# Up products with 512 columns of tokens, their halves added afterwards, and an earlier copy of the compressed keys

## The reference, cut to what matters

```python
def swiglu(h, w13, w2):
    a, b = jnp.split(h @ w13, 2, axis=-1)
    return (jax.nn.silu(a) * b) @ w2
```

## Time and profile before

| what | value |
|---|---|
| median of three runs | 1698.47 us |
| profiled execution | 1698.32 us, of which the span from the first to the last instruction is 1696.5 us |
| TensorE busy with matmuls | 1579.6 us, 93% |
| VectorE busy | 1104.0 us, 65% |
| ScalarE busy | 758.1 us, 45% |
| DMA | 327.31 MB, 193 GB/s in the mean |
| mean granted clock of TensorE | 0.966 of full |

### The profile page before, as it was taken

How to read it: one execution, slowest core, us unless ns; L and a number is a source line. 1 busy time by engine, 2 the same in 40 slices (tenths; PEclk the granted TensorE clock), 3 DMA queues, 4 the chain that set the end, 5 groups by cost and what they waited for, 6 DMA issues and landing times. The chain is left out here.

```text
span 1696.5 us, 24909 instructions
## 1 busy us (share of the span) xinstructions
PE 1579.6 (93%) x10338; PEld 1418.8 (84%) x10338; DVE 1104.0 (65%) x1571; ACT 758.1 (45%) x1144; POOL 22.9 (1%) x30
## 2 busy tenths in 40 slices
PE   5896879999999999999898999999999998989998
PEld 4684678999998999877777999889987777789986
DVE  3577655777776686568656677566776676567543
ACT  4634544343435444355535444354433655254442
POOL 0001000000000000000000000000000000000000
PEclk9998978999999999999889999999999998899999
DMA  7322324777674677544503677646775444156550
GB/s 257 112 76 111 127 100 171 283 275 292 255 285 155 234 281 273 215 166 170 184 28 122 242 267 269 255 177 244 263 283 191 160 176 149 32 187 242 173 201 35
DMA packets 56879, 327.31 MB, mean 193 GB/s; under 512 B 6448, under 2 KB 6832, under 8 KB 27312
## 3 DMA queue, kind: packets, MB, share of 16 engines
q1 hardware_dynamic: 55440, 322.76, 51.8%
q10 hardware_dynamic: 1328, 2.97, 0.5%
HBM read 324.65 MB, written 1.05 MB: 192 GB/s over the span
## 5 line engine op out<-in xcount | busy, mean ns | idle before, releaser
L286 DVE TENSOR_TENSOR wlo<-raw,whi 128x2048 fp32r<-128x2048 f32 (+2 forms) x236 | 533.8, 2265 | 281.8 <-ACT whi L281 281.6
L281 ACT ACTIVATE whi<-raw 128x2048 fp32r<-128x2048 f32 (+2 forms) x236 | 444.6, 1891 | 277.8 <-PE ps L1241 151.0
L1237 PE MATMUL ps<-hreg_r,whi 128*128 128x256 f32 x1760 | 501.0, 285 | 4.3 <-ACT mix L1286 4.3
L1241 PE MATMUL ps<-hreg_r,wlo 128*128 128x256 f32 x1760 | 500.0, 284 | 0.0
L1238 PE MATMUL ps<-hreg_r,whi 128*128 128x256 f32 x1760 | 500.0, 284 | 0.0
L1237 PEld LDWEIGHTS ps<-hreg_r,whi 128*128 128x128 f32 x1760 | 339.9, 193 | 5.7 <-ACT mix L1286 4.9
L1238 PEld LDWEIGHTS ps<-hreg_r,whi 128*128 128x128 f32 x1760 | 339.8, 193 | 0.5
L1241 PEld LDWEIGHTS ps<-hreg_r,wlo 128*128 128x128 f32 x1760 | 339.8, 193 | 0.0
L1386 PE MATMUL ps<-whi,ireg_r 128*128 128x512 f32 x480 | 187.4, 390 | 0.5 <-ACT ireg_r L1352 0.5
L1387 PE MATMUL ps<-whi,ireg_r 128*128 128x512 f32 x480 | 187.0, 390 | 0.0
L1390 PE MATMUL ps<-wlo,ireg_r 128*128 128x512 f32 x480 | 186.8, 389 | 0.0
(11 more groups left out here) (349 smaller groups left out, 1854.0 us busy)
## 6 DMA issues: line engine op xcount, KB each, us to landing
raw<-in_wu SPq DMA_DIRECT2D x230, 1024.0 KB, 5.6
adaw<-in_wada SPq DMA_DIRECT2D x144, 512.0 KB, 3.9
raw<-in_wu SPq DMA_DIRECT2D x4, 568.0 KB, 4.5
raw<-in_wu SPq DMA_DIRECT2D x2, 544.0 KB, 5.0
x<-in_x SPq DMA_DIRECT2D x2, 512.0 KB, 4.6
out<-hreg SPq DMA_DIRECT2D x2, 512.0 KB, 2.6
crow<-in_c ACTq DMA_DIRECT2D x1, 512.0 KB, 4.0
greg<-in_cst ACTq DMA_DIRECT2D x1, 512.0 KB, 8.3
```

Of the source, the lines that this page charges most:

```text
L281: act.activation(self.whi[:, m, 0:width], self.raw[:, n % NRAW, 0:width], ACT.Copy).then_inc(*self.A.done("hi", n))
L286: dve.tensor_tensor(self.wlo[:, m, 0:width], self.raw[:, n % NRAW, 0:width], self.whi[:, m, 0:width].bitcast(F32), ALU.subtract).then_inc( ...
L1237: pe.matmul(o, wh, self.hhi[:, kt, :], start=kt == 0, stop=False)
L1241: mm = pe.matmul(o, wl, self.hhi[:, kt, :], start=False, stop=kt == 7)
```

## The change

1. The upper and lower activations lie side by side, block by block: `hboth` is 8 x 512, and `hhi` and `hlo` are its halves.
2. In `up_tile` the two matmuls with `whi` become one with 512 columns. Its result has upper x upper in columns 0 to 255 of the bank and upper x lower in 256 to 511. The third matmul adds to the first half as before. Both tiles of a unit are made before the signal that it is done.
3. The two halves of the bank have to be added: ScalarE copies the second halves of both banks (`copy_act`, 128 x 512) into `sil` or `prd`, and VectorE adds the first halves to that (`sum_dve`, 128 x 512). Silu, gate, product, upper and lower part now run once for both tiles, with 512 elements, from and to SBUF. TensorE waits for the sum of the step before (`V("sum", ...)`) where it waited for silu or product.
4. The order on ScalarE and VectorE: `up_act` and `up_dve` replace the loops; the upper and lower part of a hidden product are made one step later, behind the next unit's split, and the `mod` operation is put before the split that it followed (`ada_first`).
5. `ada_table`: 1.00 per unit for the experts, 0.82 in the up units and 1.30 in the down units of a feed-forward stage; 0.60 in mixers as before. As a result the one that was due at VectorE's `ahead_dve(n0 + 14)` in either mixer is due at `ahead_dve(n0 + 15)`.
6. In `mixer_dve` the copies of the compressed keys and values stand before `ahead_dve(n0 + 14)`.

```diff
-            due += 60 if stage[n][0] == "m" else 96
+            due += 60 if stage[n][0] == "m" else 100 if stage[n][0] == "moe" else 130 if ORDER[n][0][0] == "w2" else 82
...
-        self.hhi = hr[:, 0:2048].rearrange("p (a b) -> p a b", b=256)
-        self.hlo = hr[:, 2048:4096].rearrange("p (a b) -> p a b", b=256)
+        self.hboth = hr[:, 0:4096].rearrange("p (a b) -> p a b", b=512)
+        self.hhi, self.hlo = self.hboth[:, :, 0:256], self.hboth[:, :, 256:512]
...
-            pe.matmul(o, wh, self.hhi[:, kt, :], start=kt == 0, stop=False)
-            pe.matmul(o, wh, self.hlo[:, kt, :], start=False, stop=False)
+            pe.matmul(self.ps[:, b, :], wh, self.hboth[:, kt], start=kt == 0, stop=False)
             if f == 0 and kt == 0:
                 pe.wait_ge(*V("lo", n))
-            mm = pe.matmul(o, wl, self.hhi[:, kt, :], start=False, stop=kt == 7)
+            mm = pe.matmul(self.ps[:, b, 0:256], wl, self.hhi[:, kt, :], start=False, stop=kt == 7)
...
-        for f in range(2):
-            pe.wait_ge(*A("sil", st, nth - 1, f))
-            mm = self.up_tile(pe, n, f, 4 + f)
-            mm.then_inc(*(P.done("up", st, nth, "a", 0) if f == 0 else P.done("unit", n)))
+        pe.wait_ge(*(A("sil", st, 0) if nth == 1 else V("sum", st, nth - 1, "a")))
+        self.up_tile(pe, n, 0, 4)
+        self.up_tile(pe, n, 1, 5).then_inc(*P.done("unit", n))
...
+    def up_act(self, act, name, j, st, nth, hi_before, free=None):
+        self.ahead_act(act, UNIT[name, "a", j])
+        if nth > 1:
+            self.hidden_act(act, st, nth - 1, hi_before, free)
+        self.copy_act(act, st, nth, "a", UNIT[name, "a", j], self.sil[:, nth % 2])
+        self.ahead_act(act, UNIT[name, "b", j])
+        self.silu_act(act, st, nth)
+        if nth > 2:
+            act.wait_ge(*self.V("hlo2", st, nth - 2))
+        self.copy_act(act, st, nth, "b", UNIT[name, "b", j], self.prd[:, nth % 2])
...
+    def copy_act(self, act, st, nth, part, n, to):
+        b = 4 if part == "a" else 6
+        act.wait_ge(*self.P("unit", n))
+        act.activation(to, self.ps[:, b:b + 2, 256:512], ACT.Copy).then_inc(*self.A.done("low", st, nth, part))
+
+    def sum_dve(self, dve, st, nth, part, to):
+        b = 4 if part == "a" else 6
+        dve.wait_ge(*self.A("low", st, nth, part))
+        dve.tensor_tensor(to, self.ps[:, b:b + 2, 0:256], to, ALU.add).then_inc(*self.V.done("sum", st, nth, part))
...
+    def up_dve(self, dve, name, j, st, nth, before, gate=None):
+        A, V = self.A, self.V
+        s, p = self.sil[:, nth % 2], self.prd[:, nth % 2]
+        self.ahead_dve(dve, UNIT[name, "a", j], True)
+        if nth > 1:
+            self.lower_dve(dve, st, nth - 1, *before)
+        self.sum_dve(dve, st, nth, "a", s)
+        self.ahead_dve(dve, UNIT[name, "b", j], True)
+        self.sum_dve(dve, st, nth, "b", p)
+        dve.wait_ge(*V("sum", st, nth, "b"))
         if gate is not None:
...
+            dve.tensor_tensor(p, p, gate.unsqueeze(1).to_broadcast([128, 2, 256]), ALU.mult).then_inc(*V.done("gated", st, nth))
+            dve.wait_ge(*V("gated", st, nth))
+        dve.wait_ge(*A("sil", st, nth))
+        dve.tensor_tensor(p, p, s, ALU.mult).then_inc(*V.done("prd", st, nth))
...
         maxima(7)
         probs(6)
-        self.ahead_dve(dve, n0 + 14)
         dve.wait_ge(*P("KC", st))
...
         dve.tensor_tensor(v["VC"], ps[:, 5, 64:128].unsqueeze(1).to_broadcast([128, 8, 64]),
                           self.bd.unsqueeze(2).to_broadcast([128, 8, 64]), ALU.mult).then_inc(*V.done("KC", st))
+        self.ahead_dve(dve, n0 + 14)
         self.ahead_dve(dve, n0 + 15)
```

More of the change, by code:

```diff
@@ L1327, in up_pe @@
         n = UNIT[name, "b", j]
[L1328 to L1344, removed]
@@ L1346, in hidden_act, with silu_act @@
-    def hidden_act(self, act, st, j, f, hi, free=None):
-        r = (2 * j + f) % 4
-        act.wait_ge(*self.V("prd", st, j, f))
+        pe.wait_ge(*(V("prd", st, 0) if nth == 1 else V("sum", st, nth - 1, "b")))
+        self.up_tile(pe, n, 0, 6)
+        self.up_tile(pe, n, 1, 7).then_inc(*P.done("unit", n))
+    def silu_act(self, act, st, j):
+        act.wait_ge(*self.V("sum", st, j, "a"))
+        act.activation(self.sil[:, j % 2], self.sil[:, j % 2], ACT.Silu).then_inc(*self.A.done("sil", st, j))
@@ L1398, in mhid_of, with mhid_pair @@
         return self.mhid[:, e % 2, 0, f, :], self.mhid[:, e % 2, 1, f, :]
+    def mhid_pair(self, e):
+        return self.mhid[:, e % 2, 0], self.mhid[:, e % 2, 1]
     def moe_units(self):
@@ L1495, in moe_act @@
             if e:
-                self.ahead_act(act, UNIT[("moe", e), "a", 0])
-                self.ahead_act(act, UNIT[("moe", e), "b", 0])
-                for k in range(2):
-                    self.silu_act(act, MOE, e, k)
-                for k in range(2):
-                    free = P("unit", UNIT["down", e - 2, 0]) if e >= 2 else P("gb", 7)
-                    self.hidden_act(act, MOE, e, k, self.mhid_of(e, k)[0], free)
+                free = P("unit", UNIT["down", e - 3, 0]) if e >= 3 else P("gb", 7)
+                self.up_act(act, ("moe", e), 0, MOE, e, self.mhid_pair(e - 1)[0], free)
+            if e == 15:
+                self.hidden_act(act, MOE, 15, self.mhid_pair(15)[0], P("unit", UNIT["down", 13, 0]))
             if back is not None:
@@ L1583, in moe_dve @@
             if e:
-                self.up_dve(dve, ("moe", e), 0, MOE, e)
-                for k in range(2):
-                    self.hidden_dve(dve, MOE, e, k, *self.mhid_of(e, k), gate=self.gateb[:, e, :])
+                self.up_dve(dve, ("moe", e), 0, MOE, e, self.mhid_pair(e - 1), self.gateb[:, e, :])
+            if e == 15:
+                self.lower_dve(dve, MOE, 15, *self.mhid_pair(15))
             if back is not None:
@@ L1642, in ffn_act @@
                 self.rope_tables_act(act)
-            for part in "ab":
-                self.ahead_act(act, UNIT[("ffn", l, i), part, j])
             if j == 0:
+                for part in "ab":
+                    self.ahead_act(act, UNIT[("ffn", l, i), part, j])
                 self.first_act(act, st)
             else:
-                for k in range(2):
-                    self.silu_act(act, st, j, k)
+                self.up_act(act, ("ffn", l, i), j, st, j, self.hidhi[:, 2 * j - 2:2 * j])
             if j == 1:
@@ L1652, in ffn_act @@
                     self.first_hidden_act(act, st, k, self.hidhi[:, k, :])
-            if j:
-                for k in range(2):
-                    self.hidden_act(act, st, j, k, self.hidhi[:, 2 * j + k, :])
             if j == 8:
                 self.gate_rows_act(act, st, 0)
+        self.hidden_act(act, st, 10, self.hidhi[:, 20:22])
         for j in range(8):
@@ L1683, in ffn_dve @@
                 self.rope_tables_dve(dve)
-            self.up_dve(dve, ("ffn", l, i), j, st, j)
             if j == 0:
+                for part in "ab":
+                    self.ahead_dve(dve, UNIT[("ffn", l, i), part, j])
                 self.first_dve(dve, st)
+            else:
+                k = slice(2 * j - 2, 2 * j)
+                self.up_dve(dve, ("ffn", l, i), j, st, j, (self.hidhi[:, k], self.hidlo[:, k]))
             if j == 1:
```

73 lines of the change are left out of this document (30 added, 43 removed).

## The result

The changed kernel takes 1672.29 us in the median of four runs (1668.78 to 1675.06), the kernel before 1697.94 in four beside it. The ratio is 0.9848, 95% interval 0.9826 to 0.9871: 25.7 us less, where 38 had been forecast. In a second set of runs the same two gave 0.9856 (0.9835 to 0.9878). The profiled execution of the changed kernel is the slowest of its four, 1675.06 us, of which 1672.3 are the span; before it was 1698.32 with a span of 1696.5.

The account below looks back on a forecast made before the run. TensorE's matmul count times pace was taken to bound the feed-forward and expert stages, its waits the mixers. 1698.3 - 22.9 (wide products) - 17.2 (compressed keys) + 1.1 (last expert) = 1659.3, forecast 1660 us, range 1650 to 1679.

Parts of the forecast that it names:

- A: Whole kernel: the forecast itself holds, 1660 us, own range 1655 to 1665; chance 0.50.
- B: Mixers: the clock falls behind the compressed scores although nothing waits, only 8.0 us gained there; 1668.5 us; chance 0.20.
- C: Mixers: another wait replaces the removed one, so the mixer keeps its time; 1676.5 us; chance 0.08.
- Rival E: Feed-forward steps: VectorE becomes the bound and the kernel gets slower, 1707 to 1744 us; chance 0.04.
- The wide products: Up tiles: in 1760 blocks two 256-column matmuls become one of 512, 0.227 us instead of 0.240; -22.9 us.
- Rival D: Up tiles: the wide product saves nothing, 512 followed by 256 columns keep 0.360 us; 1682 us; chance 0.08.
- The rule on the gap: Up tiles: the skill's rule has joining two matmuls save about 2.5 ns, -4.4 us; the prediction took 13 ns.
- The last expert: Last expert's down product: TensorE waits 1.6 us where it waited 0.55; +1.1 us (0 to +2).
- The compressed keys: Both mixers: earlier copies remove TensorE waits of 3.61 and 4.37 us; -17.2 us in all, 8.0 of it the waits.
- 9.2 us expected on top for the clock: Both mixers: time got back beyond the waits because TensorE runs at full clock, not half; 9.2 of the 17.2 us.
- The `mod` operations: ScalarE and VectorE: their new order was counted as nothing; VectorE's chain behind the compressed keys included one's new due time.

Follow-up runs that it names:

- in turns: The changed kernel's own order: each product of 512 columns is followed by one of 256 columns; 1672.29 us, ratio 0.9848.
- one block late: Changed kernel with each 256-column product issued one block later, behind the next block's 512-column one; one execution, 1671.53 us.
- by tile: Changed kernel with a tile's eight 512-column products first, then its eight 256-column ones; 1666.26 us, ratio 0.9813.
- two and two: Changed kernel with two 512-column products, then two 256-column ones, alternating in a tile; one execution, 1662.68 us.
- by unit: Changed kernel with all sixteen 512-column products of a unit first, then its sixteen 256-column ones; 1664.24 us, ratio 0.9811.
- second profile: The changed kernel run once more, unaltered, beside other kernels on one chip; 1672.65 us, ratio 0.9856.
- old due times: Changed kernel with the `mod` operations' due times as before the change (0.96 per unit everywhere but in mixers); 1672.24 us, ratio 0.9848.
- keys alone: Kernel before the change with only the earlier copies of the compressed keys; 1684.41 us, ratio 0.9922.
- every product wide: Changed kernel with the third product also widened to 512 columns, adding lower times lower; one execution, 1848.9 us.
- by unit, old due times: Changed kernel with a unit's 512-column products before its 256-column ones, and `mod` due times as before the change; 1661.85 us, ratio 0.9783.
- two and two, old due times: Changed kernel with two 512-column, then two 256-column products alternating, and `mod` due times as before the change; 1664.07 us, ratio 0.9798.
- dense work between: Kernel before, with early key copies and twelve 512-column projection products moved between the compressed scores and group 8's scores; 1689.5 us, ratio 0.9962.
- three edits (dense work between): Changed kernel with products grouped by unit, `mod` due times as before, and projection products between compressed scores and group 8's; 1669.63 us, ratio 0.9851.

## Why the prediction was right, and where it was not

**The number.** 1672.3 us lies in the stated range, 1650 to 1679, but not in the case that carried half of the chance (A, 1655 to 1665). It stands between B (1668.5) and C (1676.5), because two terms came at half and at seven tenths of their size. In the profiled execution, besides, 1.9 us of the gain lie ahead of the experts, where nothing was changed.

**Direction, and what bounds.** TensorE's pace and its waits in the mixers bound the kernel, and both edits shortened them. Rival E did not come: VectorE needs 82% of the time and TensorE never waits for a sum except for 0.3 us near the rotation angles. The DMA engines moved 265 and 280 GB/s where 266 and 285 were worked out.

**The wide products** were put at -22.9 us; the up products' distances fell by 11.5 us. This is the term that was mis-sized. The price of the wide product was right (0.227 with wide products alone), and so, nearly, was the sum of the two widths where they come in pairs or groups (0.348 a pair). What failed is the step that added the two paces for products in turns: 0.353 a pair in most units. The orders, in us ("long" and "short" are the profiles by the stretch at half clock in the experts):

```
order in a unit          changes of width   unit, median   sum, long      sum, short
before                   -                  5.760          638.6          637.2
in turns                 32                 5.650          627.1, 627.0   624.5
one block late           28                 5.640          -              624.4
by tile                  4                  5.587          620.1          -
two and two              16                 5.573          619.0          617.7
by unit                  2                  5.567          618.1, 618.1   -
```

Rival D's doubt, "no row has the two widths in turns", was the right one, at half its price. Shown is that the other orders are worth 7 to 9 us. Why products in turns go at 0.353 a pair stays open, and the forecast's 0.347 is not out of reach for them: three whole units of the changed kernel, three of it in the second profile and nine with the old due times have it, so something beside the order has a part in it, which no run here names.

**The rule on the gap.** Joining two products saved 12 ns by unit or two and two (16 joins take a unit from 5.760 to 5.567 or 5.573 us) and 7 ns in turns, against the 2.5 ns of "TensorE: Matmul & The Clock Gate", section "Back-to-back issue gap" (Trainium skill), whose formula is for an isolated matmul. The measurement decides; the rule would have given -4.4 us for -11.5.

**The last expert.** +1.1 us was forecast with a wait of 1.6 us; the wait is 1.58 us where the earlier trace rows have 0.55, and the stretch is 0.80 us longer:

```profile
510.12 0.47 PE L1403 MATMUL ps<-whi,ireg_r 128*128 128x512 f32 x1 [1.58 <-ACT ireg_r L1341]
```

**The compressed keys.** Both waits are gone, as forecast, in every kernel with the early copies. Of the 9.2 us expected on top for the clock, 4.2 came. The windows behind the compressed scores (L2099) in the changed kernel, layer 0 and then layer 1:

```profile
833.20:837.00 3.80, 3.80 (x33) 3.37 (x33) 3.18 (x3) 1.31 (x1) 0.00 (x0) 1.00 0.50 168
...
1408.30:1415.00 6.70, 6.70 (x26) 4.73 (x23) 6.52 (x13) 0.88 (x6) 0.00 (x0) 0.50 0.81 313
```

In layer 0 the clock stays up until 11.8 us behind the start of L2099; of the 9.1 us, 7.4 came, or 10.8 in the second profile. In layer 1 L2099 starts at 1406.11 and the clock is at half from 1408.2 for 6.8 us, though TensorE has no idle time there: rival B, with half of the old stretch and not all of it, and 4.9 us instead of 8.1. The step that failed is "with the idle time gone I expect it to stay". The reading in front of it was off too: the old fall did not come right behind the idle time but within it, 0.5 us before its end in layer 0 and 2.8 us in layer 1 (half clock from 839.9 and 1423.6, L2083 at 840.46 and 1426.45).

From the start of the compressed scores to the next fall of the clock (us, each kernel's profile):

```
                                          layer 0   layer 1
changed kernel                             11.8       2.1
changed kernel again                        3.9       2.3
keys alone                                  3.2      11.8
old due times                              12.8      12.6
by tile                                     4.1      12.2
every product wide                         11.8      19.5
by unit                                     4.7       4.1
by unit, old due times                     12.0      12.7
two and two                                 4.5       4.2
one block late                             18.8      11.8
two and two, old due times                  4.8      11.8
dense work between                          8.7      11.9
three edits (dense work between)           10.3       9.0
```

The first eleven have the same order of TensorE's work there. In 10 of their 22 mixers the clock falls within 5 us, with TensorE busy from the start of the scores to the fall; in 12 it stays for 11.8 us or longer. So the small matmuls without any idle time can be followed by a fall, and the same ones often are not. The four mixers with dense products between them have no fall within 5 us, which at 12 of 22 is too few to show that the dense products kept the clock. Two profiles of one kernel differ by 3.4 us in a mixer, so the gain of either layer can't be told more finely than that.

**The `mod` operations.** The prediction counted the new due times as nothing outside the compressed keys. They did lengthen one wait in each mixer by 1.2 us and made one of 1.7 us in layer 0, and the kernel with the old times paid about as much elsewhere. No run shows a clear difference in the whole: in turns the ratios are 0.9848 and 0.9848, by unit 0.9811 and 0.9783 with intervals that just meet, and the profiled executions of these two took 1663.73 and 1663.93 us.

## What to carry to other kernels

A pace that is read from a run of equal matmuls holds for equal neighbours. Where a change mixes two widths, the order in which they alternate is part of the price: here two and two, or all of one width first, gave 7 to 9 us on top of what the change gave, at no cost that a run shows. A wait that is removed gives back its own length only if nothing else comes to stand in its place: the two waits for the compressed keys gave their 8.0 us, the 1.2 us taken off another wait gave nothing that the whole shows. Time that hangs on the granted clock is less certain still. Here 4.2 of 9.2 us came, and the clock fell or stayed behind the same work from mixer to mixer, so one trace of one execution is not enough to count on either. Work moved in to keep the clock is no free filler when it had covered another wait.

## What was not expected of the hardware

A narrow product (256 columns) standing singly between wide ones (512) made a pair of 0.353 us in most units and of 0.347 in a few of the same kernel; two and two made 0.348; the first five wide ones behind a narrow group were 2 to 8 ns slower than the later ones. The granted clock fell to half 3.2 us after the start of a run of small matmuls in which TensorE was busy all the time (1.00 before 838.0 us, 0.50 after), and stayed at 1.00 for 11.8 us behind the same run in the next layer of the same execution.
